# The output phase of a two-layer retention/gMLP decoder takes its heads in another order, and weight loads are spread out

## The reference

```python
xn = _rmsnorm(h, norm_g)
proj = jnp.einsum('btd,de->bte', xn, w_in)
q, k, v, g_r, u, v_g, g_g = jnp.split(proj, SPLITS, axis=-1)
# retention head group: 8 heads of 128; state S carried from chunk to chunk of 128 tokens
o, S = _retention(_rope(q), _rope(k) * 128 ** -0.5, v, S0)
o = o * lax.rsqrt(jnp.mean(o * o, axis=-1, keepdims=True) + EPS)   # per head and token
o = o * jax.nn.silu(g_r)
# gMLP head group: 8 heads of 128
s = _spatial_gate(_layernorm(v_g, ln_g, ln_b), ws, bs)
m = u * s * jax.nn.silu(g_g)
# merge head groups, single output projection, residual
y = jnp.einsum('bte,ed->btd', jnp.concatenate([o, m], axis=-1), w_out)
return h + y, S, vn
```

## Time and profile before

| what | value |
|---|---|
| time, 3 runs | 1234.46 us median (1232.26 to 1235.78) |
| profiled execution | 1239.12 us; span of its slowest core, 2: 1237.6 us |
| spans of the cores | 1220.7 to 1237.6 us |
| layer 0: units, then output phase (core 2) | about 151 to 503, 505 to 642 us |
| layer 1: units, then output phase (core 2) | about 762 to 1108, 1112 to 1231 us |

### The profile page before, as it was taken

One profiled execution on the slowest core, in us unless ns is written; L12 is line 12 of the kernel. 1 busy time (PEld: TensorE's weight loads), 2 busy tenths in 40 slices (PEclk: granted clock), 3 DMA queues, 4 the chain that ended last, 5 costly groups with the idle time before them and its releaser, 6 DMA issues.

```text
span 1237.6 us, 26755 instructions; the slowest of 8 cores (1220.7 to 1237.6 us)
## 1 busy us (share of the span) xinstructions
PE 1168.0 (94%) x9333; PEld 665.9 (54%) x9490; DVE 717.9 (58%) x1416; ACT 561.6 (45%) x1014; POOL 498.0 (40%) x560
## 2 busy tenths in 40 slices
PE   4999999999999799599999999999999999998997
PEld 2454466566666456244544444666666666653453
DVE  3464476777787577334443334767876777772333
ACT  3364345655655455322222533556555655652222
POOL 1011156766766655300100111567667766650000
PEclk8999999999999899899999999999999999999999
DMA  9725516544644943937750062156346546665432
GB/s 202 181 75 104 94 30 126 114 89 100 142 93 94 105 111 110 130 128 180 195 171 18 9 113 50 49 104 144 82 101 129 112 97 103 148 150 134 149 141 104
DMA packets 142244, 139.56 MB, mean 113 GB/s; under 512 B 41760, under 2 KB 112160, under 8 KB 142112
## 3 DMA queue, kind: packets, MB, share of 16 engines
q1 hardware_dynamic: 123248, 98.25, 28.7%
q0 software_dynamic: 18432, 38.28, 20.6%
q10 hardware_dynamic: 432, 1.31, 0.3%
HBM read 124.51 MB, written 43.19 MB: 136 GB/s over the span
## 4 chain that ended last, share of the span: by engine, by line
PE 84%; ACT 5%; issue 4%; DMA 4%; POOL 2%; DVE 1%; DVEq 0%; ACTq 0%; SPq 0%; POOLq 0%
PE ps L671 30%; PE ps L579 17%; PE ps L997 17%; PE ps L715 8%; DMA VO<-cats 2%; ACT L452 1%; PE ps L750 1%; ACT B_q L452 1%; PE ps L872 1%; PE ps L830 1%; PE ps L795 1%; PE ps L538 1%; POOL kT_84 L687 1%; PE ps L768 1%; PE ps L737 1%
## 5 line engine op out<-in xcount | busy, mean ns | idle before, releaser
L452 ACT ACTIVATE B_q<-ps 64x512 f32<-64x512 f32 x128 | 75.8, 592 | 101.5 <-DVE A_q L696 59.1
L777 DVE SCALAR_TENSOR_TENSOR S_90<-S_90,ps 128x128 f32<-128x128 f32 x240 | 67.7, 282 | 37.5 <-PE ps L768 32.8
L452 ACT ACT_TABLE_LOAD x65 | 83.4, 1283 | 12.8 <-DVE rs L806 7.6
L687 POOL TENSOR_TENSOR kT_84<-A_k,B_k 128x512 bf16<-128x512 f32 x32 | 40.8, 1274 | 73.0 <-DVE B_k L685 73.0
L579 PE MATMUL ps<-wv_102,xnT 128*128 128x512 bf16 x252 | 61.0, 396 | 3.9 <-DMA wv_102<-w_v 2.9
L579 PE MATMUL ps<-wv_104,xnT 128*128 128x512 bf16 x246 | 59.9, 379 | 0.6
L579 PE MATMUL ps<-wv_105,xnT 128*128 128x512 bf16 x251 | 59.9, 379 | 0.3
L804 DVE TENSOR_TENSOR og<-ps,sgr_97 128x512 f32<-128x512 f32 x32 | 22.1, 692 | 61.2 <-ACT sq L452 61.2
L592 DVE CAST VO<-ps 128x512 bf16<-128x512 f32 x32 | 22.1, 692 | 60.7 <-PE ps L579 60.7
L579 PE MATMUL ps<-wv_103,xnT 128*128 128x512 bf16 x250 | 57.1, 379 | 0.3
L452 ACT ACTIVATE sq<-ps 128x512 f32<-128x512 f32 x64 | 38.2, 596 | 40.8 <-PE ps L798 40.0
(11 more groups left out here) (389 smaller groups left out, 3031.7 us busy)
## 6 DMA issues: line engine op xcount, KB each, us to landing
stt_109<-st SPq DMA_DIRECT2D x16, 512.0 KB, 4.8
stt_110<-st SPq DMA_DIRECT2D x16, 512.0 KB, 4.2
ss_out<-stt_109 SPq DMA_DIRECT2D x16, 512.0 KB, 3.4
ss_out<-stt_110 SPq DMA_DIRECT2D x16, 512.0 KB, 10.1
hb_51<-xp SPq DMA_DIRECT2D x8, 512.0 KB, 4.8
hb_53<-xp SPq DMA_DIRECT2D x8, 512.0 KB, 5.4
cats<-catn_95 SPq DMA_DIRECT2D x16, 256.0 KB, 2.9
cats<-catn_96 SPq DMA_DIRECT2D x16, 256.0 KB, 4.3
```

What stands on the lines that cost most here:

```text
L452: P.add("act", lambda e: e.activation(out=out, in_=in_, func=func, **kw), r, w, t_act(n) + (0.2 if "accum_out" in kw else 0), tset=tset)
L687: pool(lambda e: e.tensor_tensor(out=dst[:], in0=A_k[:], in1=B_k[:], op=ALU.add), A_k.k() + B_k.k(), dst.k(), 512)
L777: return e.scalar_tensor_tensor(out=S32[:, c, :], in0=S32[:, (c + 3) % 4, :], scalar=_C["sdec"][h], in1=src, op0=ALU.mult, op1=ALU.add)
```

## The change

- The eight w_out groups are taken, loaded and placed in the ring in the order `JO = [4, 5, 6, 7, 0, 1, 2, 3]`: gMLP heads first, retention heads 6 and 7 last.
- Ahead of the loop over chunks, the first seven groups of chunks 0, 1 and 2 are issued (`o_front`, 21 groups in six PSUM banks); then each of those chunks gets its last group in `o_chunk`.
- In the last head (h = 7) the normalisation, the store and the transpose are done for each unit (512 tokens), not for each pair.
- From head 1 on, head weights are loaded two after unit q = 0 and one after each of q = 1, 2, 3, where five were loaded after q = 3. The first five w_out tiles are tied to the end of units 24, 25, 26, 28, 29; the other three stay as they were.
- The prompt state has two tiles, used by heads in turn (2 KB more a partition).
- The planner reckons a DMA transpose at 2.5 times its bytes.

```diff
+JO = [4, 5, 6, 7, 0, 1, 2, 3]
+WO_AT = [24, 25, 26, 28, 29]
...
-        S32 = T("S32", [128, 4, 128], F32)
+        S32a = T("S32a", [128, 4, 128], F32)
...
+        S32s = [S32a, T("S32b", [128, 4, 128], F32)]
...
-... semkey=key, nbytes=nbytes,
+... semkey=key, nbytes=2.5 * nbytes,
...
-            for j in range(8):
+            for j in JO:
                 wo_of[(l, j)] = (pos % 16) // 2
...
+            S32 = S32s[h % 2]
...
-            if u.n % 2:
-                act(rs[:], rs[:], AF.Ln, rs.k() + small.k(), rs.k(), 8, tset="le", scale=1.0 / 128, bias=Ecol(h))
-                act(rs[:], rs[:], AF.Exp, rs.k(), rs.k(), 8, tset="le", scale=-0.5)
+            if u.n % 2 or h == H - 1:
+                js = (u.n % 2,) if h == H - 1 else (0, 1)
+                j0, n = js[0], len(js)
+                ra, rk = rs[:, j0:j0 + n, :], rs.k((j0, j0 + n))
+                act(ra, ra, AF.Ln, rk + small.k(), rk, 8, tset="le", scale=1.0 / 128, bias=Ecol(h))
+                act(ra, ra, AF.Exp, rk, rk, 8, tset="le", scale=-0.5)
...
+                t0 = (u.q - n + 1) * 512
+                src = cats[h, t0 // 1024][:, j0 * 512:(j0 + n) * 512]
+                names = [("cats", h, t0 // 1024, j) for j in js]
+                dma("sp", src, cn[:, j0:j0 + n, :].rearrange("p j d -> p (j d)"), cn.k((j0, j0 + n)), names, (cn.name, j0), 131072 * n)
+                dma_t(VO[:, h, t0:t0 + n * 512].rearrange("p (c i) -> p c i", c=4 * n), src,
+                      names, VO.k(h, (t0, t0 + n * 512)), "catT", 131072 * n)
...
+        obanks = {}
+
+        def o_front(l, c):
+            obanks[c] = (orot(), orot())
+            o_mm(l, c, obanks[c], cat_ap(c), cat_k(c), 128, JO[:7])
+
         def o_chunk(l, c):
-            banks = (orot(), orot())
             h = hb[c % 4]
-            o_mm(l, c, banks, cat_ap(c), cat_k(c), 128, range(8))
+            if c not in obanks:
+                o_front(l, c)
+            banks = obanks.pop(c)
+            o_mm(l, c, banks, cat_ap(c), cat_k(c), 128, JO[7:])
...
-                        for it in witems[wi:min(wi + 5, 40)]:
-                            w_item(l, it, after=[mark["p"]])
-                        wi = min(wi + 5, 40)
+                if h > 0:
+                    for it in witems[wi:min(wi + 1 + (u.q == 0), 40)]:
+                        w_item(l, it, after=[mark["p"]])
+                    wi = min(wi + 1 + (u.q == 0), 40)
+                if n in WO_AT:
+                    w_item(l, witems[40 + WO_AT.index(n)], after=[mark["p"]])
...
-            for it in witems[40:]:
+            for it in witems[45:]:
                 w_item(l, it)
...
+            for c in range(3):
+                o_front(l, c)
             for c in range(NCH):
```

More of the change, by code:

```diff
@@ L382, in build_nc @@
         fing = T("fing", [128, D], F32, at=t_at)
-        s_at = cur[0]
+        S32s = [S32a, T("S32b", [128, 4, 128], F32)]
         stt = [T("stt%d" % i, [128, 8, 128], F32) for i in range(2)]
@@ L466, in dma_t @@
         def dma_t(out, in_, r, w, key, nbytes):
-            lastT[key] = P.add("sp", lambda e: e.dma_start_transpose(out=out, in_=in_), r, w, semkey=key, nbytes=nbytes,
+            lastT[key] = P.add("sp", lambda e: e.dma_start_transpose(out=out, in_=in_), r, w, semkey=key, nbytes=2.5 * nbytes,
                                after=[lastT[key]] if key in lastT else ())
@@ L807, in OO @@
                 sq.k(), rs.k(u.n % 2), 512)
-            if u.n % 2:
-                act(rs[:], rs[:], AF.Ln, rs.k() + small.k(), rs.k(), 8, tset="le", scale=1.0 / 128, bias=Ecol(h))
-                act(rs[:], rs[:], AF.Exp, rs.k(), rs.k(), 8, tset="le", scale=-0.5)
+            if u.n % 2 or h == H - 1:
[4 more added lines that the diff above has]
+                act(ra, ra, AF.Exp, rk, rk, 8, tset="le", scale=-0.5)
                 cn = catn[u.n // 2 % 2]
-                for j in range(2):
+                for j in js:
                     pool((lambda j: lambda e: e.tensor_tensor(
@@ L961, in mm @@
                         kk = 2 * j + k2
-                        r = e.matmul(ps[:, b, :], cf(kk), w[:, k2, half * 512:(half + 1) * 512], start=(kk == 0), stop=(kk == 15))
+                        r = e.matmul(ps[:, b, :], cf(kk), w[:, k2, half * 512:(half + 1) * 512], start=(kk == 8), stop=(kk == 7))
                     return r
@@ L997, in mm @@
                             r = e.matmul(ps[0:n, banks[half], :], cat_fn(kk), w[:, k2, half * 512:(half + 1) * 512],
-                                         start=(kk == 0), stop=(kk == 15))
+                                         start=(kk == 8), stop=(kk == 7))
                     return r
@@ L1085, in build_nc @@
                     ev.setdefault(p, []).insert(0, (norm_back, c))
-            witems = [("h", h, g) for h in range(H) for g in range(5)] + [("o", j) for j in range(8)]
+            witems = [("h", h, g) for h in range(H) for g in range(5)] + [("o", j) for j in JO]
             steps = [(i, c) for c0 in (0, 4) for i in range(2) for c in range(c0, c0 + 4)] + [(2, c) for c in range(8)]
```

4 lines of the change are left out of this document (removed).

## The result

| | before | after |
|---|---|---|
| median of 4 runs, side by side | 1235.12 us | 1217.28 us (1216.24 to 1218.29) |
| profiled execution; span of its slowest core | 1239.1; 1237.6 us | 1217.0; 1214.7 us |

The ratio is 0.985, 95% interval 0.982 to 0.988: 17.8 us less. The prediction said 1215. Runs in which the cores of one die stood at a lower clock than the others are left out of all medians and ratios here.

What follows compares the result with a forecast made beforehand. TensorE, 94% busy, was taken to bound the kernel apart from holes. Core 7's span 1222.1 - 10.4 = 1211.7, plus 1.5 and new costs of 0.9 + 1 + 0.5, gave 1215.6, stated as 1215; 8-in-10 range 1207 to 1226.

Steps and rivals of the forecast that it cites:

- B: Layer 0, start of output phase: TensorE idles 12.52 us for head 7's late transpose, then slow clock costs 2.85; -15.4 us claimed.
- C: Layer 1, start of output phase: 3.05 us idle, then four groups at slow clock; closing it claimed to save 4.75 us.
- A: Layer 0, head 6: a jam of three w_out loads and a slow transpose loses 8.9 us on core 2; claimed to go.
- chain of core 6: Layer 0, head 6: VectorE waits 7.3 us for `sp_out`, ScalarE's state copy for VectorE, TensorE 6.4 us; second tile removes it.
- core 2's stall: Layer 0, head 6: TensorE waits 6.8 us ahead of a gate matmul, ending for no recorded reason.
- w_out tiles: Output phase: front reaches the sixth and seventh tiles early, slack 2.5 us; cost taken as 1, bounds 0 or 9.0 plus 2.85.
- Rival 1: Layer 0 output phase: front stands on a w_out tile in the jam after 5 groups; +10.9 us, 1226; chance 0.13.
- Chunk 0's norm: Output phase: next layer's transposes of chunk 0 may wait for its normed rows; 0.5 us, bounds 0 and 2.
- rival 4: Both output phases: three small transposes keep w_out loads slow; 28.7 us idle and slow clock a layer, 1267; chance 0.04.
- Rivals 2 to 4: The second: ScalarE sets the pace in head 7, all 12.6 us exposed, 1227, chance 0.06; rival 3 and rival 4 listed separately.
- rival 3: Layer 0, head 6: one load a unit still holds up some wait, so 8.9 us stay; 1224; chance 0.06.

## Why the prediction was right, and where its sum was off

**Order and front: right, except "and, with it, its slow clock".** The idle of 12.52 and of 3.05 us went, no core waits for `VO`, and 21 groups run 0.86 apart. But I took the slow clock for a result of B's long idle alone. The changed kernel has it in both layers without that idle, and core 2 has it once more in layer 1 (0.50 from 1157 to 1160 us), behind the small matmuls of the sample group. Its price by the timeline of layer 0: the two groups take 0.39 and 0.14 us more than 0.86, the gate matmuls between them 0.19 more than 0.23, and the unit's output matmuls 0.35 more: 1.1 us. By the length of the phase, with it and without it, it is 1.5 (122.1 and 120.6). Of C's 4.75, core 2 got 2.2; of B's 15.4, 14.1.

**Halves: the price was sought on the wrong engine.** I took four more waits of 0.2 us for silu, 0.9 in all. There are still 13 of them, before and after 43.5 us apart, so once a head and not at each switch. ScalarE got four table loads more, not eight (65 before, 69 now; 6.0 us more busy, not 12.6), and paces nothing. The price is on GpSimd, which I had only counted for DMA issues: 1.43 us of wait a layer where 0.3 stood, about half of it won back at the next wait (0.73 where 1.27 stood). Whether the lower clock behind it belongs to that price stays open, as does the whole price: the medians with halves and with pairs differ by less than their runs do. Of the Trainium skill's rule that I weighed ("ScalarE: Activation LUTs", What ACT_TABLE_LOAD costs), the load of 1283 ns agrees with the profile, where the loads take 1283 ns as a mean; the drain did not show: four more loads, with their Ln and Exp, made ScalarE 6.0 us more busy.

**And the halves were not needed.** I wrote that the front covers the transpose "even if it stays as late". That held: with pairs it takes up to 18.7 us to land and nothing waits.

**Two tiles and spread loads: right on A.** A's 8.9 came as 8.8. The tile costs nothing; the spread loads cost 0.4 us in the units of layer 0 (336.3, where a core before that met no hole took 335.9). On the chain of core 6 they do the same work twice, which I didn't see: either alone cuts it. On core 2's stall they don't: the spread loads end it, the tile alone does not.

What TensorE waited for in that stall no record names, and no run tests it. The trace has a lead that I had overlooked. Among the DMAs of a core is a queue that it calls "instruction". On core 2 it has a single packet between 394 and 426 us, of another queue number, and the next one of queue 8 starts at 426.45 and has landed at 427.42, 1.5 us before TensorE goes on. The two windows, 394 to 426 and 426 to 429 us, and TensorE:

```profile
q14 instruction: 1, 0.01, 0.1%
```
```profile
q8 instruction: 1, 0.02, 2.0%
```
```profile
428.92 0.59 PE L830 MATMUL ps<-WT_143,VM 128*128 128x128 bf16 x4 [6.77 <-issue]
```

All runs together have eight such stalls over 1 us, all in kernels with the burst of loads and the transposes. Each ends 1.3 to 2.8 us after a packet of queue 8 has landed, six of them 1.3 to 1.5 us after it, and the packet of that queue before it had landed 22 to 34 us earlier, the longest time at the longest stall. So TensorE may have stood for want of instructions that came late in the jam. The transpose, which landed 0.09 us before TensorE went on, is hardly what it waited for: in four of the other seven stalls the transpose of that place lands only after TensorE has gone on.

**w_out tiles: mis-sized, on the safe side.** I took a slack of 2.5 us for the seventh tile and a cost of 1. Issued at 490.91, it landed after 7.3 us, at 498.2, and was first read at 505.32: 7.1 us. The load was 2.5 us faster than the 9.8 that I took from a jam, it was issued 6.8 and not 6.2 us ahead of the phase, and the phase's first groups were slower. Rival 1 needs more than that; it appears only when both front and halves are taken out, on four cores.

**Chunk 0's norm: taken at 0.5, measured 0.** The transposes at 525.39 and 529.29 us ran without a wait.

**The sum.** Predicted for the slowest core: a span of 1211.7 + 2.4 = 1214.1, and 1.5 around it. Measured: 1214.7, and 2.3 around it. That is near for the wrong reasons in part: the 2.4 of new costs were w_out tiles, silu and chunk 0's norm, none of which came; the lower clock in both layers and the wait for `qT` took their place. And of the 10.4 that I took off core 7, 4.55 were a slow clock borrowed from core 2. Core 7 got none of that back: its granted clock is 0.992 before and after. It gained 7.4, and 2.3 of these lie ahead of the first unit, where nothing was changed (its first `P_gr` matmul starts at 154.9 us before and at 152.6 after). So that 1214.1 met 1214.7 is in part luck. Two of the other sums do not come out as written: the upper end of 1220 is not what the upper bounds of the small costs add up to (0.9, 11.85 and 2 on 1211.7 + 1.5 make 1228), and rival 4's 1267 stands on the profiled run, where 1215 was given for the median. Of the 2.3 us from 1215 to 1217.28, 0.6 is the span, 0.8 what lies around it, 0.6 I had rounded away, and 0.3 lies between the profiled run and the median. In the span is also the last store, which lands 3.8 us after its issue on core 2 (1214.4 - 1210.6) where it took 2.6 (1237.6 - 1234.97); why stays open. Core 2 no longer decides, as predicted. Rivals 2 to 4 are ruled out by the changed kernel's own profile: the units take 336.6 us on every core, there is no hole near 420 us, and the loads land sooner, not later. What rival 3 says is real without the spread loads: the run with the front alone has A, and the run with the tile alone has the stall without a recorded reason.

## What to carry to other kernels

When a wait is removed, look at what the clock does behind the smaller waits that are left, before booking the lower clock as gone with it, and look over the whole stage: a lower clock that is missing at its start may only come later. When a piece of work is split so that it is ready sooner, list what stands behind each piece on every engine that runs it, not only on the engine that the piece is costliest on. A store that is late for one tile can be cured by a second tile or by fewer loads beside it: test each alone, and look at every core and layer, before keeping both or dropping one.

## What the runs showed of the hardware

- A DMA transpose beside loads that cast (loads without a cast were not tried): 256 KB take 18.7 us there, against 3.0 at best. With a plain copy in its place two loads beside it take 9.6 us as median, where they take 14.3 with it, and the core's DMA engines move 201 GB/s, where they move 68 at as full a share. The Trainium skill ("Advanced Engine Details and Errata", X-Bar Transpose (TRN2)) has transposes as fast as other DMAs on TRN2. At best the two are near each other here, 3.0 us and 2.4 for a plain copy; beside these loads the measurement differs, and it decides.
- The start of an output phase at the lower clock level (0.59 over 4.2 us, 1.2 GHz for most of them): on all eight cores of the changed kernel, behind a wait of 1.43 us and one of 0.73 with four matmuls between. Behind 0.29 and 1.28 us at the same place it is missing on all eight cores with pairs in head 7, and there on five of eight with halves in units 28 and 29. What decides between these stays open.
- With pairs, seven cores of eight have the lower level at the end of 128 matmuls of 16 columns, in 9 us in which TensorE was busy throughout (0.50 behind 1.00).
- Eight stalls of TensorE without a recorded reason, 1.2 to 6.8 us, each ended 1.3 to 2.8 us after a packet of the DMA queue "instruction" had landed. That the one makes the other is not shown.
